# Flipping the first layer's input before its norm: the gain in the copies, the roots behind the projections

## The chip, the cores and the metric

The kernel runs on one core of a Trainium2 chip. A core has TensorE (matrix products into PSUM, weights loaded by LDWEIGHTS), VectorE, ScalarE, GpSimd, and SyncE, which here only issues transfers. The metric is the device time of one execution in microseconds; lower is better.

## What is computed

Two layers of a decoder trunk on 256 tokens of width 1024, in float32. Only the front of layer 0 is touched:

```python
def rms_norm(x, g):
    xf = x.astype(jnp.float32)
    y = xf * lax.rsqrt(jnp.mean(xf * xf, axis=-1, keepdims=True) + EPS)
    return (y * g.astype(jnp.float32)).astype(x.dtype)
...
def hybrid_mixer(h, positions, w_in, ...):
    u = h @ w_in
    ...
    a_out = stick_breaking_attention(sb[:, :, 0], sb[:, :, 1], sb[:, :, 2])
    b_out = conformer_conv(cv[..., :CV_WIDTH], cv[..., CV_WIDTH:], ...)   # val * sigmoid(gate), then a convolution
    q = rope(dl[:, :, 0], positions)
    k = rope(dl[:, :, 1], positions)
    c_out = dilated_mixture(q, k, dl[:, :, 2])
    return jnp.concatenate([a_out, b_out, c_out], axis=-1) @ w_out
...
    for l in range(DEPTH):
        y = hybrid_mixer(rms_norm(h, mix_norm_pre[l]), positions, w_in[l], ...)
        h = h + rms_norm(y, mix_norm_post[l])
        ...  # cross-attention into 256 memory tokens, then a gated ConvFFN
```

The norm's factor splits in two: a root per token and a gain per feature.

## The kernel before

Each engine has its own hand-written program; they meet by semaphores, and each runs its program strictly in the order written. Weights come as 512 KB groups (128 x 1024) through a ring of four: SyncE loads `raw`, ScalarE copies it to `whi` (rounded, L567), VectorE makes `wlo = raw - whi` (L993), and TensorE forms every product in three passes: high by high, high weights by low input, low weights by high input. ScalarE and VectorE run three groups ahead of TensorE, and a group's slot is free again when TensorE has used it.

The start of layer 0, for token tile 0 and then 1 (128 tokens each): ScalarE sums the squares (`squares_x`, L579), VectorE and GpSimd make the root (`st(S_HRS + t)`, one value per partition, since tokens lie on the partitions), TensorE spreads the gain over the partitions by two products (L1626), VectorE multiplies x by root and gain (`first_scale`, L1070), TensorE transposes the result by halves of 512 features (`flip`, L1595) so that features lie on the partitions, ScalarE copies the high part out of PSUM (`first_input_hi`, L589) and VectorE subtracts for the low part (`first_input_lo`, L1075). `idle_products` (L1620) are products of zeros whose result nobody reads. Then come 24 calls of `first_pass` of two products each (L1858), the projection for the dilated q (weight groups 0 to 3).

After it TensorE works through the convolution's value and gate (features on partitions, `transposed_product`, L1665 to L1667; groups 4 to 7), half of the memory's keys (8 to 11), the dilated k and v (`product`, L1648 to L1650; 12 to 19), the stick-breaking q and k (features on partitions, 20 to 23) and v. Between them VectorE prepares the memory, the angles (`angles`), the gated value (L1336, after ScalarE's sigmoid L759), rotates q and k (`rope`, L1218 to L1224), and runs the convolution's 31 taps per half (`conv_taps`, L1273) whenever nothing else is due. The stick-breaking q and k leave PSUM through ScalarE (`transposed_in`, L675) into `sbT`, and `sb_scores` (L1813) uses them next. TensorE's transposes of the convolution (L1968) wait for the last taps.

## Time and profile before

| | us |
|---|---|
| median of three runs | 821.71 |
| lowest, highest | 821.61, 821.96 |
| profiled execution, its span | 820.0 |
| outside its span, by the median | 1.7 |
| TensorE busy | 809.4 |
| VectorE busy | 654.8 |
| ScalarE busy | 528.0 |
| GpSimd busy | 29.2 |

The profile is one execution; the times of its rows count from the start of its span. An engine's busy time is no bound by itself: what counts is which wait ends last in each stretch. A row's duration is that of one instruction or of several merged ones ("x4"); neighbours on an engine overlap by some hundredths of a microsecond. In brackets stands how long the engine was idle before the row, and what released it.

### The profile page before, as it was taken

To read this page: it belongs to the slowest core of one execution; us is meant where nothing else is said; L and a number is where in the kernel's file an instruction comes from. 1 tells how busy PE (TensorE), PEld (TensorE's weight loads), DVE (VectorE), ACT (ScalarE), POOL (GpSimd) and SP (SyncE) were. 2 spreads that over 40 slices of the span, in tenths; PEclk is the share of its full clock that TensorE was granted. 3 is DMA by queue.
4 is the path that set the end of the run, shared out by engine and by line. 5 is a ranking of instruction groups with operands and counts; after the bars stand their busy time and mean duration, and the time that the engine had idled before them with its cause. 6 is when DMAs were issued, how large, how long until landed. Compare 5 with 4: busy or idle time off the path is not lost.

```text
span 820.0 us, 12147 instructions
## 1 busy us (share of the span) xinstructions
PE 809.4 (99%) x4636; PEld 698.3 (85%) x4636; DVE 654.8 (80%) x1149; ACT 528.0 (64%) x823; POOL 29.2 (4%) x54
## 2 busy tenths in 40 slices
PE   8999999999999999999999999999999999999997
PEld 5998888889888888888899889888988888888885
DVE  6899996777776899998387999948788489999753
ACT  5656886567556777765365588756766477776541
POOL 2100000010010000000010000001000000000000
PEclk9999999999999999999999999999999999999999
DMA  8755345473464566556656443456635545555651
GB/s 298 284 178 182 103 129 167 142 259 101 155 233 140 167 206 196 178 191 214 197 201 237 147 154 108 137 168 208 202 121 178 190 129 180 193 176 196 228 184 52
DMA packets 40446, 145.72 MB, mean 178 GB/s; under 512 B 4594, under 2 KB 4738, under 8 KB 40388
## 3 DMA queue, kind: packets, MB, share of 16 engines
q1 hardware_dynamic: 38448, 138.38, 51.4%
q0 software_dynamic: 1936, 6.55, 2.3%
q8 instruction: 37, 0.61, 0.3%
q14 instruction: 21, 0.17, 0.1%
q10 hardware_dynamic: 4, 0.00, 0.0%
HBM read 143.87 MB, written 1.05 MB: 177 GB/s over the span
## 4 chain that ended last, share of the span: by engine, by line
PE 87%; DVE 7%; ACT 3%; issue 1%; DMA 0%; DVEq 0%; POOLq 0%; POOL 0%; ACTq 0%
PE acc L1682 8%; PE psCD L1682 4%; PE acc L1648 4%; PE acc L1649 4%; PE acc L1650 4%; PE acc L1692 4%; PE psAB L1682 4%; PE acc L1745 3%; PE psAB L1648 3%; PE psAB L1650 3%; PE psAB L1649 3%; PE acc L1747 3%; PE acc L1746 3%; PE psCD L1595 3%; PE acc L1665 3%; PE acc L1666 2%
## 5 line engine op out<-in xcount | busy, mean ns | idle before, releaser
L993 DVE TENSOR_TENSOR wlo<-raw,whi 128x1024 fp32r<-128x1024 f32 x240 | 288.1, 1222 | 68.7 <-ACT whi L567 67.1
L567 ACT ACTIVATE whi<-raw 128x1024 fp32r<-128x1024 f32 x240 | 249.4, 1057 | 119.3 <-PE acc L1650 44.1
L1682 PE MATMUL acc<-xT,whi 128*128 128x512 f32 x288 | 89.0, 390 | 0.0
L1682 PEld LDWEIGHTS acc<-xT,whi 128*128 128x128 f32 x288 | 54.1, 188 | 11.8
L1536 DVE SCALAR_TENSOR_TENSOR KT<-V,par,KT 128x255 f32<-128x255 f32 (+1 forms) x144 | 60.0, 480 | 2.1 <-ACT KT L926 1.5
L1692 PE MATMUL acc<-xT,wlo 128*128 128x256 f32 x288 | 58.0, 283 | 0.0
L1273 DVE SCALAR_TENSOR_TENSOR arena<-arena,par 128x256 f32<-128x256 f32 x120 | 50.3, 481 | 0.8 <-ACT arena L767 0.8
L1665 PE MATMUL acc<-xT,whi 128*128 128x256 f32 x176 | 50.9, 289 | 0.0
L1682 PE MATMUL psCD<-xT,whi 128*128 128x512 f32 x160 | 50.0, 393 | 0.0
L1666 PE MATMUL acc<-xT,whi 128*128 128x256 f32 x176 | 49.7, 283 | 0.0
L1667 PE MATMUL acc<-xT,wlo 128*128 128x256 f32 x176 | 49.7, 283 | 0.0
L494 POOL TENSOR_TENSOR stat<-stat 128x1 f32<-128x1 f32 x30 | 18.8, 626 | 775.9 <-DVE stat L1133 401.3
L1692 PEld LDWEIGHTS acc<-xT,wlo 128*128 128x128 f32 x288 | 44.8, 191 | 0.0
L1682 PE MATMUL psAB<-xT,whi 128*128 128x512 f32 x128 | 39.7, 391 | 0.0
L926 ACT ACTIVATE KT<-V,par 128x256 f32<-128x256 f32 x72 | 37.3, 595 | 0.7 <-DVE V L1522 0.7
L1665 PEld LDWEIGHTS acc<-xT,whi 128*128 128x128 f32 x176 | 33.6, 191 | 2.9 <-issue 2.7
L617 ACT ACTIVATE junk<-acc 128x512 bf16<-128x512 f32 x20 | 11.8, 592 | 37.0 <-PE acc L1766 22.6
L1648 PE MATMUL psAB<-whi,gT 128*128 128x512 f32 x88 | 34.2, 389 | 0.0
L1649 PE MATMUL psAB<-wlo,gT 128*128 128x512 f32 x88 | 34.2, 389 | 0.0
L1650 PE MATMUL psAB<-whi,gT 128*128 128x512 f32 x88 | 34.2, 389 | 0.0
L1666 PEld LDWEIGHTS acc<-xT,whi 128*128 128x128 f32 x176 | 33.7, 191 | 0.1
L1667 PEld LDWEIGHTS acc<-xT,wlo 128*128 128x128 f32 x176 | 33.7, 191 | 0.0
(328 smaller groups left out, 2084.8 us busy)
## 6 DMA issues: line engine op xcount, KB each, us to landing
raw<-stream_dram SPq DMA_DIRECT2D x256, 512.0 KB, 4.2
gpost<-gain_dram POOLq DMA_DIRECT2D x6, 512.0 KB, 5.3
gpre<-gain_dram POOLq DMA_DIRECT2D x5, 512.0 KB, 6.2
memn<-mem_dram SPq DMA_DIRECT2D x2, 512.0 KB, 10.3
out_dram<-h SPq DMA_DIRECT2D x4, 256.0 KB, 2.0
cst<-const_dram SPq DMA_DIRECT2D x1, 896.0 KB, 6.1
h<-x_dram SPq DMA_DIRECT2D x2, 256.0 KB, 2.8
h<-x_dram SPq DMA_DIRECT2D x1, 512.0 KB, 8.2
```

Of the source, the lines that this page charges most:

```text
L567: act.activation(home(g)[0], raw[:, s * GW:(s + 1) * GW], ACT.Copy).then_inc(w_hi.sem, 1)
L993: dve.tensor_tensor(lo, raw[:, cols], hi.bitcast(F32), ALU.subtract).then_inc(w_lo.sem, 1)
L1273: e = dve.scalar_tensor_tensor(acc, src, w, acc, ALU.mult, ALU.add)
L1536: e = dve.scalar_tensor_tensor(y[:, c, shift:SEQ], u[:, 0:SEQ - shift], par[:, PC_FW + 3 * fc + 1 - k:PC_FW + 3 * fc + 2 - k], y[:, c, shi ...
L1648: pe.matmul(outs[t], a_hi, whi[:, cols], start=k == 0, stop=False)
L1649: pe.matmul(outs[t], a_hi, wlo[:, cols], start=False, stop=False)
L1650: e = pe.matmul(outs[t], a_lo, whi[:, cols], start=False, stop=k == k_of - 1)
L1665: pe.matmul(dst, whi[:, cols], hi[:, toks], start=k == 0 and c % 2 == 0, stop=False)
L1666: pe.matmul(dst, whi[:, cols], lo[:, toks], start=False, stop=False)
L1667: e = pe.matmul(dst, wlo[:, cols], hi[:, toks], start=False, stop=k == KC - 1 and c % 2 == 1)
L1682: e = pe.matmul(up_halves(j, c), whi[:, cols], both, start=k == 0, stop=k == KC - 1)
L1692: e = pe.matmul(up_halves(j, c)[:, 0:SEQ], wlo[:, cols], hi, start=False, stop=False)
```

## The change

TensorE transposes x itself, neither scaled by the root nor by the gain. The gain comes in as 8 rows of 128, is turned into eight columns by one small product, and each column (one value per feature, so per partition) is the scale of a copy of 128 columns: four scaled copies on ScalarE and four scaled subtractions on VectorE take the place of one each. The roots are put in behind the projections: as a scale per partition where tokens lie on partitions (the dilated v and the stick-breaking v, by ScalarE's copies; the dilated q and k, by angles that VectorE scales beforehand), and as a row spread over all partitions where features do. That row is made by VectorE (`roots_diagonal`), TensorE (`spread_roots`) and VectorE again (`root_row`); VectorE multiplies the gate by it before the sigmoid and the value after, and GpSimd multiplies all of `sbT` by it. The squares of x move behind the first four weight splits. SyncE issues the first weight group second, ScalarE issues the constants' head, and there are seven and five idle products where there were four and two. TensorE's order in the first passes changes too. Layer 1 stays as it was.

```diff
...
+        root_row = gpre[:, 0:SEQ]
+        trig0 = gpre[:, SEQ:SEQ + TOK * 2 * HALF]
+        gain0 = gpre[:, SEQ + TOK * 2 * HALF:SEQ + TOK * 2 * HALF + KC]
+        by_token = lambda n: root_row.unsqueeze(1).to_broadcast([P, n, SEQ])
...
+            def first_rows(n):
                 sp_.dma_start(h[:, n * NT:(n + 1) * NT], x[0:P, n * NT:(n + 1) * NT]).then_inc(x0_in[n].sem, 16)
-            sp_.dma_start(cst[:, 0:CC_TRI], consts[:, 0:CC_TRI]).then_inc(head_in.sem, 16)
+
+            first_rows(0)
             group(0)
+            first_rows(1)
...
-                pool.wait_ge(xn_ready.sem, xn_ready.at(l, 2 * TOK))
+                if l:
+                    pool.wait_ge(xn_ready.sem, xn_ready.at(l, 2 * TOK))
+                else:
+                    pool.wait_ge(root_row_in.sem, 1)
+                    pool.wait_ge(sbT_raw.sem, 2)
+                    pool.tensor_tensor(sbT, sbT, by_token(4), ALU.mult).then_inc(sbT_in.sem, 2)
+                    pool.wait_ge(gpad_in.sem, 1)
+                    pool.wait_ge(k_roped.sem, TOK)
+                    pool.wait_ge(sbT_in.sem, 2)
                 gain(gpre, gpre_in, l, X_PRE)
...
+                act.wait_ge(gain0_cols.sem, 1)
                 act.wait_ge(xt_tr.sem, 2 * t + b + 1)
-                act.activation(x_chunks(0, b, t), blocks(psCD[b]), ACT.Copy).then_inc(xt_hi.sem, 1)
-
-            act.wait_ge(gain0_room.sem, 1)
-            act.dma_start(gain0[0:2, :], gains[0, MIX_PRE, :].rearrange("(n c) -> n c", n=2)).then_inc(gain0_in.sem, 16)
+                for c in range(4):
+                    e = act.activation(x_chunks(0, b, t)[:, c], blocks(psCD[b])[:, c], ACT.Copy,
+                                       scale=gain0[:, 4 * b + c:4 * b + c + 1])
+                e.then_inc(xt_hi.sem, 1)
+
+            act.dma_start(gain_rows, gains[0, MIX_PRE, :].rearrange("(k p) -> k p", p=P)).then_inc(gain0_in.sem, 16)
+            act.dma_start(cst[:, 0:CC_TRI], consts[:, 0:CC_TRI]).then_inc(head_in.sem, 16)
             act.wait_ge(half_set.sem, 1)
             own.link(act.activation(junk[:, 0:1], st(S_POW), ACT.Sin))
-            squares_x(0)
+            first_input_hi(0, 0)
             split_group(0, 0)
+            first_input_hi(0, 1)
+            split_group(0, 1)
             for b in range(2):
-                first_input_hi(0, b)
-            split_group(0, 1)
-            squares_x(1)
+                first_input_hi(1, b)
             split_group(0, 2)
             split_group(0, 3)
-            for b in range(2):
-                first_input_hi(1, b)
+            squares_x(0)
...
-                act.activation(sig, accs[1][1][:, :], ACT.Sigmoid).then_inc(cv_sig.sem, 1)
+                if l:
+                    act.activation(sig, accs[1][1][:, :], ACT.Sigmoid).then_inc(cv_sig.sem, 1)
+                else:
+                    act.wait_ge(gate_scaled.sem, 1)
+                    act.activation(sig, sig, ACT.Sigmoid).then_inc(cv_sig.sem, 1)
...
-                    act.activation(dlv[:, t * NT:(t + 1) * NT], accs[1][t][:, :], ACT.Copy).then_inc(dlv_in.sem, 1)
+                    if not l:
+                        act.wait_ge(h_rs.sem, t + 1)
+                    act.activation(dlv[:, t * NT:(t + 1) * NT], accs[1][t][:, :], ACT.Copy,
+                                   scale=1.0 if l else st(S_HRS + t)).then_inc(dlv_in.sem, 1)
...
-                act.activation(sbv, accs[1][0][:, :], ACT.Copy).then_inc(sbv_in.sem, 1)
+                for t in range(TOK):
+                    rows_t = slice(t * SB_W, (t + 1) * SB_W)
+                    e = act.activation(sbv[:, rows_t], accs[1][0][:, rows_t], ACT.Copy, scale=1.0 if l else st(S_HRS + t))
+                e.then_inc(sbv_in.sem, 1)
...
-            def first_scale(t, n):
-                cols = slice(t * D + n * NT, t * D + (n + 1) * NT)
-                dve.wait_ge(gain0_spread.sem, n + 1)
-                dve.wait_ge(h_rs.sem, t + 1)
-                dve.scalar_tensor_tensor(xn[:, cols], h[:, cols], st(S_HRS + t),
-                                         psAB[n], ALU.mult, ALU.mult).then_inc(xn_ready.sem, 1)
-
             def first_input_lo(t, b):
                 dve.wait_ge(xt_hi.sem, 2 * t + b + 1)
-                dve.tensor_tensor(x_chunks(1, b, t), blocks(psCD[b]), x_chunks(0, b, t).bitcast(F32),
-                                  ALU.subtract).then_inc(xt_lo.sem, 1)
-
-            norm_input(0, 0, 0)
-            for n in range(2):
-                first_scale(0, n)
+                for c in range(4):
+                    e = dve.scalar_tensor_tensor(x_chunks(1, b, t)[:, c], blocks(psCD[b])[:, c],
+                                                 gain0[:, 4 * b + c:4 * b + c + 1],
+                                                 x_chunks(0, b, t)[:, c].bitcast(F32), ALU.mult, ALU.subtract)
+                e.then_inc(xt_lo.sem, 1)
+
+            def roots_diagonal(t):
+                dve.wait_ge(head_in.sem, 16)
+                dve.wait_ge(h_rs.sem, t + 1)
+                dve.tensor_scalar(diag[:, t * P:(t + 1) * P], ident, st(S_HRS + t), None,
+                                  ALU.mult).then_inc(diag_set.sem, 1)
+
+            def first_angles_scaled():
+                dve.wait_ge(trig_ready.sem, 1)
+                for t in range(TOK):
+                    cols = slice(2 * t * HALF, 2 * (t + 1) * HALF)
+                    own.link(dve.tensor_scalar(trig0[:, cols], trig[:, cols], st(S_HRS + t), None, ALU.mult))
+
+            dve.wait_ge(gain0_tr.sem, 1)
+            dve.tensor_copy(gain0, psAB[0][:, 0:KC]).then_inc(gain0_cols.sem, 1)
+            dve.wait_ge(gain0_cols.sem, 1)
+            first_input_lo(0, 0)
             split_group(0, 0)
-            first_input_lo(0, 0)
+            first_input_lo(0, 1)
             split_group(0, 1)
-            norm_input(0, 0, 1)
-            first_input_lo(0, 1)
-            for n in range(2):
-                first_scale(1, n)
+            for b in range(2):
+                first_input_lo(1, b)
             split_group(0, 2)
             split_group(0, 3)
-            for b in range(2):
-                first_input_lo(1, b)
+            for t in range(TOK):
+                norm_input(0, 0, t)
...
+                        roots_diagonal(t)
...
+                    dve.wait_ge(root_spread.sem, 1)
+                    dve.tensor_copy(root_row, psAB[1][:, 0:SEQ]).then_inc(root_row_in.sem, 1)
...
-                dve.wait_ge(cv_sig.sem, cv_sig.at(l, 1))
-                dve.tensor_tensor(gpad[:, :, CV_K - 1:CV_K - 1 + SEQ],
-                                  accs[1][0][:, :].rearrange("p (c n) -> p c n", c=2),
-                                  sig.rearrange("p (c n) -> p c n", c=2), ALU.mult).then_inc(gpad_in.sem, 1)
+                by_half = lambda a: a.rearrange("p (c n) -> p c n", c=2)
+                gated_rows = gpad[:, :, CV_K - 1:CV_K - 1 + SEQ]
+                if l:
+                    dve.wait_ge(cv_sig.sem, cv_sig.at(l, 1))
+                    dve.tensor_tensor(gated_rows, by_half(accs[1][0][:, :]), by_half(sig), ALU.mult).then_inc(gpad_in.sem, 1)
+                else:
+                    dve.wait_ge(root_row_in.sem, 1)
+                    dve.wait_ge(w_used.sem, w_used.at(l, g_cv + PER_TILE))
+                    dve.tensor_tensor(by_half(sig), by_half(accs[1][1][:, :]), by_token(2), ALU.mult).then_inc(gate_scaled.sem, 1)
+                    own.link(dve.tensor_tensor(gated_rows, by_half(accs[1][0][:, :]), by_token(2), ALU.mult))
+                    dve.wait_ge(cv_sig.sem, cv_sig.at(l, 1))
+                    dve.tensor_tensor(gated_rows, gated_rows, by_half(sig), ALU.mult).then_inc(gpad_in.sem, 1)
...
+                    first_angles_scaled()
                     rope(0, qr, g_dlq + PER_TILE, q_roped)
...
-            def first_input(b):
-                pe.wait_ge(xn_ready.sem, b + 1)
-                flip(psCD[b], xn[:, b * NT:(b + 1) * NT]).then_inc(xt_tr.sem, 1)
+            def first_input(t, b):
+
+                pe.wait_ge((x1_in if t else x0_in[b]).sem, 16)
+                if t:
+                    pe.wait_ge(xt_lo.sem, b + 1)
+                flip(psCD[b], h[:, t * D + b * NT:t * D + (b + 1) * NT]).then_inc(xt_tr.sem, 1)
 
             def idle_products(n):
 
                 for i in range(n):
-                    pe.matmul(accs[1][0][:, :], idle[:, 0:P], idle[:, :], start=True, stop=True)
-
-            idle_products(4)
-            pe.wait_ge(spread_set.sem, 1)
+                    pe.matmul(accs[1][0][:, :], idle[:, :], idle[:, :].unsqueeze(1).to_broadcast([P, NT // P, P]),
+                              start=True, stop=True)
+
+            def spread_roots():
+
+                pe.wait_ge(ones_set.sem, 1)
+                for t in range(TOK):
+                    pe.wait_ge(diag_set.sem, t + 1)
+                    e = pe.matmul(psAB[1][:, t * P:(t + 1) * P], ones0, diag[:, t * P:(t + 1) * P], start=True, stop=True)
+                e.then_inc(root_spread.sem, 1)
+
+            idle_products(7)
+            pe.wait_ge(head_in.sem, 16)
             pe.wait_ge(gain0_in.sem, 16)
-            for n in range(2):
-                pe.matmul(psAB[n], pick[:, n * P:(n + 1) * P], gain0, start=True,
-                          stop=True).then_inc(gain0_spread.sem, 1)
-            pe.wait_ge(head_in.sem, 16)
-            first_input(0)
-            idle_products(2)
-            first_input(1)
+            pe.matmul(psAB[0][:, 0:KC], gain_rows, ident[0:KC, 0:KC], start=True, stop=True).then_inc(gain0_tr.sem, 1)
+            first_input(0, 0)
+            idle_products(5)
+            first_input(0, 1)
...
                     first_pass(both_hi, 0, 0)
+                    first_pass(low_x, 0, 0)
                     first_pass(low_w, 0, 0)
-                    first_pass(low_x, 0, 0)
                     first_pass(both_hi, 1, 0)
                     first_pass(low_x, 1, 0)
                     first_pass(low_w, 1, 0)
+                    for b in range(2):
+                        first_input(1, b)
                     first_pass(both_hi, 2, 0)
                     first_pass(low_x, 2, 0)
-                    first_pass(both_hi, 3, 0)
-                    first_pass(low_x, 3, 0)
-                    inputs(0, 1)
                     first_pass(both_hi, 0, 1)
                     first_pass(both_hi, 1, 1)
                     first_pass(low_w, 2, 0)
+                    first_pass(both_hi, 3, 0)
+                    first_pass(low_x, 3, 0)
+                    first_pass(both_hi, 2, 1)
                     first_pass(low_w, 3, 0)
-                    first_pass(both_hi, 2, 1)
                     first_pass(both_hi, 3, 1)
...
+                    spread_roots()
                     transposed_product(g_cv + 2, 2, X, acc[1], k0=4)
+                    pe.wait_ge(root_row_in.sem, 1)
...
```

How the order of instructions moves, at three places (line numbers are those of each version; the names are the code's, `acc0` and `acc1` being the two PSUM sets; what an instruction waits for stands in brackets).

ScalarE, at the start; before:

```order
L579 ACTIVATE junk,stat<-h 128x512 [waits x0_in1]
L567 ACTIVATE whi<-raw 128x1024 [waits w_used,raw_in0]
L589 ACTIVATE xT<-psCD 128x4x128 [waits xt_tr] x2
L567 ACTIVATE whi<-raw 128x1024 [waits w_used,raw_in1]
L579 ACTIVATE junk,stat<-h 128x512 [waits x1_in] x2
L567 ACTIVATE whi<-raw 128x1024 [waits w_used,raw_in2]
L567 ACTIVATE whi<-raw 128x1024 [waits w_used,raw_in3]
L589 ACTIVATE xT<-psCD 128x4x128 [waits xt_tr] x2
```

and after:

```order
L612 ACTIVATE xT<-psCD,gpre 128x128 [waits xt_tr,gain0_cols,act_chain]
L612 ACTIVATE xT<-psCD,gpre 128x128 x3
L588 ACTIVATE whi<-raw 128x1024 [waits w_used,raw_in0]
L612 ACTIVATE xT<-psCD,gpre 128x128 [waits xt_tr,gain0_cols]
L612 ACTIVATE xT<-psCD,gpre 128x128 x3
L588 ACTIVATE whi<-raw 128x1024 [waits w_used,raw_in1]
L612 ACTIVATE xT<-psCD,gpre 128x128 [waits xt_tr,gain0_cols]
L612 ACTIVATE xT<-psCD,gpre 128x128 x3
L612 ACTIVATE xT<-psCD,gpre 128x128 [waits xt_tr,gain0_cols]
L612 ACTIVATE xT<-psCD,gpre 128x128 x3
L588 ACTIVATE whi<-raw 128x1024 [waits w_used,raw_in2]
L588 ACTIVATE whi<-raw 128x1024 [waits w_used,raw_in3]
```

The copies of token tile 1 stood behind the splits of groups 2 and 3 and now stand ahead of them; the squares are gone from this piece. On TensorE, after, the transposes of tile 1 (L1647) that these copies wait for stand behind the products with the low weights of group 1:

```order
L1919 MATMUL acc0<-whi,xT 128x512 [waits xt_hi,w_hi]
L1919 MATMUL acc0<-whi,xT 128x512
L1919 MATMUL acc0<-whi,xT 128x512 [waits xt_lo,w_hi]
L1919 MATMUL acc0<-whi,xT 128x512
L1919 MATMUL acc0<-wlo,xT 128x512 [waits xt_hi,w_lo]
L1919 MATMUL acc0<-wlo,xT 128x512
L1647 MATMUL psCD<-cst,h 128x128 [waits xt_lo,x1_in]
L1647 MATMUL psCD<-cst,h 128x128 x3
L1647 MATMUL psCD<-cst,h 128x128 [waits xt_lo,x1_in]
L1647 MATMUL psCD<-cst,h 128x128 x3
L1919 MATMUL acc0<-whi,xT 128x512 [waits xt_hi,w_hi]
```

Before, they stood behind the products with the high weights of group 3.

VectorE, at the gate of the convolution; before:

```order
L993 TENSOR_TENSOR wlo<-raw,whi 128x1024 [waits w_hi,par_in]
L1336 TENSOR_TENSOR arena<-acc1,arena 128x2x256 [waits cv_sig]
L993 TENSOR_TENSOR wlo<-raw,whi 128x1024 [waits w_hi]
L1218 TENSOR_TENSOR arena<-acc0,trig 128x512 [waits w_used,trig_ready]
L1219 TENSOR_TENSOR arena<-acc0,trig 128x512
```

and after:

```order
L1025 TENSOR_TENSOR wlo<-raw,whi 128x1024 [waits w_hi,par_in]
L1386 TENSOR_TENSOR arena<-acc1,gpre 128x512 [waits w_used,root_row_in]
L1387 TENSOR_TENSOR arena<-acc1,gpre 128x2x256
L1389 TENSOR_TENSOR arena<-arena 128x2x256 [waits cv_sig,dve_chain]
L1025 TENSOR_TENSOR wlo<-raw,whi 128x1024 [waits w_hi]
L1116 TENSOR_SCALAR gpre<-trig,stat 128x64 [waits trig_ready]
L1116 TENSOR_SCALAR gpre<-trig,stat 128x64 [waits dve_chain]
L1257 TENSOR_TENSOR arena<-acc0,gpre 128x512 [waits w_used,trig_ready,dve_chain]
L1258 TENSOR_TENSOR arena<-acc0,gpre 128x512
```

On ScalarE, after, the table load for the sigmoid has a wait for the first of them:

```order
L588 ACTIVATE whi<-raw 128x1024 [waits w_used,raw_in2]
L777 ACTIVATE trig<-trig 128x128 [waits trig_arg]
L788 ACT_TABLE_LOAD [waits gate_scaled]
L788 ACTIVATE arena<-arena 128x512 [waits w_used]
L588 ACTIVATE whi<-raw 128x1024 [waits w_used,raw_in3]
```

One product became three, with ScalarE's sigmoid between the first and the last, and two scalings of angles stand ahead of the rotation (L1257).

GpSimd, ahead of the load of the next gains; before:

```order
L490 DMA par<-param_dram 128x246
L491 DMA pww<-pw_dram 128x512
L487 DMA gpost<-gain_dram 128x1024 [waits mem_gains_tr]
L487 DMA gpre<-gain_dram 128x1024 [waits xn_ready]
L494 TENSOR_TENSOR stat<-stat 128x1 [waits ln_ms] x2
```

and after:

```order
L503 DMA par<-param_dram 128x246
L504 DMA pww<-pw_dram 128x512
L500 DMA gpost<-gain_dram 128x1024 [waits mem_gains_tr]
L544 TENSOR_TENSOR arena<-arena,gpre 128x1024 [waits sbT_raw,root_row_in]
L500 DMA gpre<-gain_dram 128x1024 [waits sbT_in,k_roped,gpad_in]
L507 TENSOR_TENSOR stat<-stat 128x1 [waits ln_ms] x2
```

A product of 128 x 1024 on `sbT` is new, and the load behind it waits for it, for the rotated k and for the gated value, since it overwrites the roots' row and the scaled angles.

## Rows read from the trace of the kernel before

**Rows 1.** The page, busy times: engine, us, share of the span, instructions.
```profile
PE 809.4 (99%) x4636; PEld 698.3 (85%) x4636; DVE 654.8 (80%) x1149; ACT 528.0 (64%) x823; POOL 29.2 (4%) x54
```

**Rows 2.** Stretches: length, busy us (instructions) per engine, granted clock, DMA share, GB/s.
```profile
50.00:100.00 50.00, 50.00 (x332) 42.64 (x331) 48.15 (x149) 35.36 (x67) 0.00 (x0) 1.00 0.48 157
```

**Rows 3.** Timeline, TensorE: start us, us, engine line op out<-in, count [idle before].
```profile
1.94 1.49 PE L1620 MATMUL acc<-idle 128*128 128x512 f32 x3
...
2.37 1.06 PE L1620 MATMUL acc<-idle 128*128 128x512 f32 x2
...
7.73 1.06 PE L1595 MATMUL psCD<-cst,xn 128*128 128x128 f32 x4
...
10.11 0.71 PE L1858 MATMUL acc<-whi,xT 128*128 128x512 f32 x2
...
23.01 0.61 PE L1858 MATMUL acc<-wlo,xT 128*128 128x512 f32 x2
23.46 0.61 PE L1858 MATMUL acc<-whi,xT 128*128 128x512 f32 x2
```

**Rows 4.** The chain that ended last: start us, us, what.
```profile
123.21 0.49 DVE arena L1273
123.74 0.55 PE psCD L1968 x3
```

**Rows 5.** Groups of ScalarE by shape: busy us, mean ns | idle before.
```profile
L669 ACT ACTIVATE xT<-psCD 128x512 fp32r<-128x512 f32 x20 | 10.9, 597 | 19.3 <-PE psCD L1595 19.3
...
L696 ACT ACTIVATE arena<-arena,stat 128x128 f32<-128x128 f32 x8 | 3.2, 402 | 3.1 <-DVE stat L1250 3.1
```

**Rows 6.** SyncE's issues in the timeline; DMA: KB each, median us to landing.
```profile
1.65 0.42 SPq L463 DMA_DIRECT2D cst<-const_dram  x1
...
3.06 0.43 SPq L459 DMA_DIRECT2D h<-x_dram  x1
...
cst<-const_dram SPq DMA_DIRECT2D x1, 80.0 KB, 3.5
...
h<-x_dram SPq DMA_DIRECT2D x1, 512.0 KB, 8.2
```

**Rows 7.** Timeline, ScalarE, the splits of the first groups.
```profile
8.27 1.06 ACT L567 ACTIVATE whi<-raw 128x1024 fp32r<-128x1024 f32 x1 [3.36 <-DMA raw<-stream_dram]
...
13.06 1.99 ACT L567 ACTIVATE whi<-raw 128x1024 fp32r<-128x1024 f32 x2
```

**Rows 8.** Timeline, ScalarE and VectorE, around the gate and the rotation of q.
```profile
39.11 1.28 ACT L759 ACT_TABLE_LOAD   x1
...
36.26 0.42 DVE L1008 TENSOR_SCALAR arena<-cst,arena 128x64 f32<-128x64 f32 x2
...
41.03 0.69 DVE L1336 TENSOR_TENSOR arena<-acc,arena 128x512 f32<-128x512 f32 x1 [0.54 <-ACT arena L759]
...
46.90 0.42 DVE L1224 TENSOR_TENSOR arena<-arena 128x256 f32<-128x256 f32 x1
```

**Rows 9.** Timeline, TensorE's flip of q; VectorE's maxima; the next scores.
```profile
49.15 1.04 PE L1595 MATMUL psCD<-cst,arena 128*128 128x128 f32 x8
...
76.66 0.17 DVE L1237 TENSOR_SCALAR stat<-stat 128x2 f32<-128x2 f32 x1
...
77.09 0.27 PE L1793 MATMUL psAB<-arena 64*128 64x128 f32 x1
```

**Rows 10.** Timeline, ScalarE's copies of q and k, TensorE's first use.
```profile
94.76 1.09 ACT L675 ACTIVATE arena<-acc 128x512 f32<-128x512 f32 x2
...
96.19 0.71 PE L1813 MATMUL psAB<-arena 64*128 64x256 f32 x4
```

**Rows 11.** Groups of GpSimd by shape: busy us, mean ns | idle before.
```profile
L494 POOL TENSOR_TENSOR stat<-stat 128x1 f32<-128x1 f32 x30 | 18.8, 626 | 775.9 <-DVE stat L1133 401.3 <-DVE stat L1415 202.1 <-DVE stat L1169 117.5
...
L497 POOL MEMSET idle<- 128x512 f32 x1 | 0.5, 529 | 0.0
...
L496 POOL MEMSET stat<- 128x1 f32 x1 | 0.1, 98 | 0.3 <-POOLq L2245 0.3
```

38 lines of the change are left out of this document (21 added, 17 removed).

## The prediction

> **What bounds the kernel now.** I read the page's busy times first, then the stretches, then the timelines of the first 50 us by engine, then the chain. TensorE is busy for 99% of the span [rows 1], so a change elsewhere counts only where it moves an instruction for which TensorE waits. VectorE is the other engine to watch: in 50 to 100 us it is busy for 48.15 of 50 us, as TensorE is for all 50 [rows 2]. In the timeline of TensorE the reader is to see that it has slack only at the start. The first pass, 48 products of 512 columns, goes from 10.11 us to 23.9 us, 0.45 behind the start of its last row; at the pace of its last rows (0.45 us for two, 0.227 for one) the 48 need 10.9 us and the eight transposes between them some 1.0 us, so about 2 us of it is waiting or a low clock [rows 3]. From there on TensorE has no idle time that a faster start would not simply shift. The chain shows the second tight place: at 123.7 us TensorE's transposes of the convolution start at the very end of VectorE's last taps [rows 4]. What delays VectorE before that delays the end.
>
> **Part 1, the start.** Removed: the spreading products, the first scaling, and the squares of x from between the weight splits. Added: each copy of a flipped half is four scaled copies of 128 columns. The copy of 512 columns takes 0.60 us; a scaled one of 128 columns takes 0.40 from SBUF [rows 5]. Neighbours overlap by about 0.09, and a source in PSUM saves about 0.03, so four cost 3 x 0.28 + 0.37, and push the next one back by 1.12 us where a plain copy took 0.50.
>
> The constants' head was issued at 1.65 us and took 3.5 us [rows 6]. ScalarE no longer waits for a memset before its issues, so I put this one at about 1.3 and its landing at 4.8 (4.2 at best). Seven idle products, 0.43 apart [rows 3], fill TensorE until about 4.3 from 1.1, the memset before them being shorter. The gain's small product and four transposes at the low clock (four took 1.06 [rows 3], some 0.85 up to the next) give 6.0 for the first flip. Then ScalarE goes: copies until 7.1, split of group 0 (1.06 for one, 0.96 as a step [rows 7]) until 8.1; its weights are issued about 1 us sooner and land about then, where ScalarE had waited 3.36 us for them until 8.27 [rows 7]. The flip of half 1 stands behind five idle products: 6.0 + 2.1 + 0.85 = 8.95 at the low clock, 7.6 at the high one. Copies, then the split of group 1: done at 11.1 (10.3).
>
> Here is the step that decides. ScalarE must now do both copies of token tile 1 before it splits group 2, and TensorE flips that tile only after the low weights of group 1: VectorE's subtraction 1.22, two products 0.45, four transposes 0.45. So ScalarE is idle for about 2.1 us, until 13.2 (12.4), then 2 x 1.12 of copies and 0.96 of split: group 2 at 16.4 (15.6), where it was ready at 14.1 [rows 7]. Behind it stand 36 products in the new order, 36 x 0.227 = 8.2. The first pass ends at 24.6 (23.8) against 23.9: **+0.5 us**. A floor that no shorter step lifts is the landing of x's second tile, issued at 3.06 and landed 8.2 later, at 11.26 [rows 6]; issued 0.5 sooner it gives 10.8 + 0.4 + 2.24 + 1.06 + 8.2 = 22.9, or -1.0. The ceiling is +1.2.
>
> **Part 2, the gate.** Before, the table load and the sigmoid followed the sine, and VectorE's gating product started at 41.03 [rows 8]. Now ScalarE first waits for VectorE's scaled gate, and the table load (1.28) stands behind that wait. VectorE had been idle for 0.54 by then [rows 8], and with the overlap of neighbours could have started at 40.40; now it is 0.35 later, for the copy of the roots' row (256 columns; a row of that size takes 0.42 [rows 8]). So: 40.75 + 0.69 for the scaled gate, 1.28, 0.63 for the sigmoid (512 columns, as a plain copy, and from SBUF), small gaps: gating at 43.44, 2.4 us later than before. The scaled value half hides in that wait. The two scalings of the angles cost 0.42, as two of 64 columns do [rows 8]. VectorE is **2.8 us late** at the end of the rotation of q, whose last row starts at 46.90 and takes 0.42: 47.32 becomes 50.1, while TensorE flips q at 49.15 [rows 8, 9]. Two products that spread the roots are also on TensorE, 0.3 to 0.6 us (its eight transposes take 1.04 [rows 9]); they are covered by this lag. The lag doesn't go away: VectorE has no idle time up to 75 us. It reaches TensorE in steps, at the latest at the score products, where the maxima end at 76.83 and the product that waits for them starts at 77.09 [rows 9]: slack 0.2. Term: **+2.6 us**. If the table load ran ahead of its wait, 1.3 us less: lower bound 1.3, upper 2.8. The roots' diagonals hide in idle time of VectorE before 28 us.
>
> **Part 3, the stick-breaking scores.** GpSimd multiplies the transposed q and k, 128 x 1024, after ScalarE's copies and before TensorE may use them. The copies end at 95.85, TensorE's first use is at 96.19 [rows 10]: slack 0.34. No such operation is in the trace. On GpSimd a 128x1 product takes 0.63 on average, and a memset of 512 columns 0.43 more than one of a single column, so 0.86 per 1024 elements for one stream [rows 11]. One stream would give 1.5, three (two reads, a write) 3.2; I take two reads as the pace: 2.35. Less the slack: **+2.1 us**, bounds 1.1 and 2.9. Behind the wait stand the scores, the value products, a flip and all of the second half of k's memory product; VectorE's mask and ScalarE's softplus wait for the scores, then come the taps whose end TensorE awaits at 123.7 [rows 4]. So it is paid in full.
>
> The Trainium skill (GPSIMD Engine Reference, Performance versus the Vector engine) gives 4497 ns for a two-input product of 2048 columns on GpSimd, by which this one would be an estimated 2.25 us and the sum 0.1 us smaller. The same page (Specifications) says that GpSimd's way to SBUF is contended by VectorE instructions with two SBUF inputs, as the taps are; no row here shows it.
>
> **Part 4.** Scaled copies of v in two pieces, on ScalarE's stretch of the chain: **+0.2 us**. The scaled dilated values cost as much and are covered by VectorE's split. The load of the next gains goes later, to about 100 us, and is wanted at 156.
>
> **Sum.** 0.5 + 2.6 + 2.1 + 0.2 = 5.4 on a span of 820.0. The median of the runs is 821.7, so 1.7 lies around the profiled span. That gives 827.1; I say 827.0.
>
> **Rivals.**
> 1. *The start pays.* If the first copies are fast and the second tile comes early, the split of group 2 follows group 1 directly, ScalarE's order alone gives 13.1 to 13.4 for it, and the pass ends at 21.3 to 21.6, 2.5 us sooner. This rival also needs the later waits hidden, up to the spreading products: 821.7 - 2.5 + 0.45 = 819.7. Against it: the floor of 22.9 above. It wins only if the later waits add less than 0.8 us.
> 2. *One of the two waits is covered.* Either the lag of VectorE or the product on GpSimd is worth little, the start is even or better: 821.7 + 2.1 + 0.2 - 0.5 = 823.5, or within 0.2% with a start of -1.0.
> 3. *TensorE falls to its low clock* while it is idle from 13.7 to 16.4. In the trace a product of 512 columns is 0.43 from the next at the start and 0.227 later [rows 3], the paces of the two levels, 1.2 and 2.4 GHz; the low one lasted to about 10 us, and TensorE is nowhere idle for so long afterwards. Eight to sixteen slow products: 1.6 to 3.2 us more, 829.5. The Trainium skill (TensorE: Matmul & The Clock Gate, What's actually happening) says that the throttled state is the default and activity releases it; by that this idle time could bring it back.
>
> **How the numbers follow.** The forecast holds 0.60, the one-wait-covered case 0.20 (half of it within 0.2%), the start that pays 0.10, low clock 0.07, and 0.03 for no difference by other ways. Faster by over 0.2% is below 820.1, slower is above 823.4; 0.2% is about what a measurement of this kernel can tell from no change. Faster 0.10, same 0.13, slower 0.77. The range: my low bounds give -1.0 + 1.3 + 1.1 + 0.1 = 1.5, or 823.2, and I go on to 822.0 for part of the second case; the high ones 1.2 + 2.8 + 2.9 + 0.3 = 7.2, or 828.9, and with a little of the third 829.3. Below it lies about 0.14, above it 0.05.
>
> **What would show it.** Right: group 2's split on ScalarE starts after 14.5; TensorE's last first-pass product ends at 23.5 to 25; the second table load starts right behind VectorE's scaled gate, at about 41.5; the flip of q waits for VectorE; TensorE waits about 2 us for GpSimd near 100 us; VectorE's last taps end at 127 to 129. Wrong: a first pass that ends before 22.5; a product on GpSimd under 1 us; or idle time of VectorE between 50 and 120 us that swallows the lag.

## The result

The changed kernel takes **830.75 us** (median of 6 runs, 829.70 to 835.64) against 821.66 of the kernel before: a ratio of 1.0122, 95% interval 1.0107 to 1.0136. Four more runs of it, beside other kernels, gave 831.12 to 833.94, ratio 1.0136 (1.0122 to 1.0150). It is slower by 9 us or more, where +5.3 was forecast, and above the range's end of 829.3. The profiled execution took 829.70 us, with a span of 827.7 against 820.0: **+7.7 us**. So there are two things to explain: 7.7 us in a trace where 5.4 were summed, and other runs that are 0.1 to 6 us longer than the one in that trace.

### The profile page after: what moved, and what is told of

Same layout as the page of the kernel before. It is cut to its first block, busy times and chain, and to the rows that moved or that the text cites. A ratio compares the mean times of both kernels' runs of the same rounds, so it can differ in the third digit from the quotient of the medians.

```text
span 827.7 us, 12197 instructions
## 1 busy us (share of the span) xinstructions
PE 810.8 (98%) x4644; PEld 700.9 (85%) x4644; DVE 657.4 (79%) x1161; ACT 531.1 (64%) x837; POOL 31.7 (4%) x55
## 4 chain that ended last, share of the span: by engine, by line
PE 78%; DVE 13%; ACT 5%; issue 2%; DMA 0%; POOL 0%; ACTq 0%; DVEq 0%; POOLq 0%
PE acc L1743 8%; DVE wlo L1025 5%; PE psCD L1743 4%; PE acc L1753 4%; PE psAB L1743 4%; PE acc L1709 4%; PE acc L1710 4%; PE acc L1711 4%; PE acc L1806 3%; PE psAB L1711 3%; PE psAB L1709 3%; PE psAB L1710 3%; PE acc L1808 3%; PE acc L1807 3%; DVE arena L1312 3%; PE psCD L1753 2%
## 5 line engine op out<-in xcount | busy, mean ns | idle before, releaser
L1312 DVE SCALAR_TENSOR_TENSOR arena<-arena,par 128x256 f32<-128x256 f32 x120 | 52.4, 498 | 0.8 <-ACT arena L796 0.8
```

Of the source, the lines that this page charges most:

```text
L1312: e = dve.scalar_tensor_tensor(acc, src, w, acc, ALU.mult, ALU.add)
```

## The profile after

The page's busy times of the changed kernel first (engine, us, share, instructions); [rows 1] answers to it.

```profile
PE 810.8 (98%) x4644; PEld 700.9 (85%) x4644; DVE 657.4 (79%) x1161; ACT 531.1 (64%) x837; POOL 31.7 (4%) x55
```

TensorE has 1.4 us more work than before, so most of the 7.7 us is idle time. Three stretches of the changed kernel show where (length, busy us of TensorE, its weight loads, VectorE, ScalarE and GpSimd, granted clock, DMA share, GB/s); [rows 2] answers to the second.

```profile
0.00:50.00 50.00, 44.37 (x277) 39.31 (x278) 33.37 (x72) 32.23 (x58) 6.51 (x16) 1.00 0.69 247
50.00:100.00 50.00, 49.45 (x316) 41.55 (x314) 48.20 (x145) 33.12 (x62) 0.00 (x0) 1.00 0.49 154
100.00:140.00 40.00, 37.31 (x263) 32.36 (x262) 36.62 (x64) 29.45 (x41) 4.31 (x4) 1.00 0.44 135
```

The same stretches of the kernel before, the first and the third:

```profile
0.00:50.00 50.00, 47.41 (x293) 39.93 (x293) 37.67 (x69) 31.07 (x48) 7.31 (x17) 1.00 0.73 261
...
100.00:140.00 40.00, 39.93 (x256) 34.47 (x255) 33.32 (x56) 31.25 (x40) 1.11 (x2) 1.00 0.49 146
```

TensorE's idle time grew by 3.0 us in the first, 0.55 in the second, 2.6 in the third. The granted clock is 1.00 in all of them. For the opening 10 us that column is to be read with care: in both kernels it gives 1.00, while the products of 512 columns there stand 0.43 us or more apart and later ones 0.227. What level the opening runs at is seen from the pace of its products.

**The start**, in the changed kernel's timeline of TensorE (start us, us, engine line op, tiles, count [idle before]):

```profile
5.82 1.11 PE L1647 MATMUL psCD<-cst,h 128*128 128x128 f32 x4
6.59 2.48 PE L1675 MATMUL acc<-idle 128*128 128x512 f32 x5
8.87 1.05 PE L1647 MATMUL psCD<-cst,h 128*128 128x128 f32 x4
...
14.08 1.04 PE L1647 MATMUL psCD<-cst,h 128*128 128x128 f32 x8
17.95 2.11 PE L1919 MATMUL acc<-whi,xT 128*128 128x512 f32 x8 [2.83 <-ACT whi L588]
```

and of ScalarE and VectorE at the same place:

```profile
11.20 1.13 DVE L1101 SCALAR_TENSOR_TENSOR xT<-psCD,gpre,xT 128x128 fp32r<-128x128 f32 x4 [0.62 <-ACT xT L612]
...
14.77 2.18 ACT L612 ACTIVATE xT<-psCD,gpre 128x128 fp32r<-128x128 f32 x8 [2.66 <-PE psCD L1647]
...
16.79 2.05 ACT L588 ACTIVATE whi<-raw 128x1024 fp32r<-128x1024 f32 x2
```

ScalarE stands idle for 2.66 us until tile 1 is flipped, copies it, and only then splits group 2; TensorE waits 2.83 us for that and goes on at 17.95. The first product behind the first pass, which started at 23.91 before, starts at 26.24: **+2.3 us**.

**The gate**: ScalarE, then VectorE, of the changed kernel; [rows 8] answer to it.

```profile
43.21 1.28 ACT L788 ACT_TABLE_LOAD   x1 [1.67 <-DVE arena L1386]
...
42.45 0.68 DVE L1386 TENSOR_TENSOR arena<-acc,gpre 128x512 f32<-128x512 f32 x1
...
45.24 0.69 DVE L1389 TENSOR_TENSOR arena<-arena 128x512 f32<-128x512 f32 x1 [1.51 <-ACT arena L788]
...
51.62 0.42 DVE L1263 TENSOR_TENSOR arena<-arena 128x256 f32<-128x256 f32 x1
```

The gating product starts 4.2 us later than before (41.03) and the rotation of q ends 4.7 later (46.90 is the row before). Of these, 2.0 were there when VectorE came to the gate: its split ahead of it started at 41.30 against 39.27.

**The stick-breaking scores**: ScalarE's copies, GpSimd, TensorE, VectorE; [rows 10] answer to the first and third.

```profile
99.48 1.09 ACT L700 ACTIVATE arena<-acc 128x512 f32<-128x512 f32 x2
...
100.75 2.62 POOL L544 TENSOR_TENSOR arena<-arena,gpre 128x1024 f32<-128x1024 f32 x1 [70.32 <-ACT arena L700]
...
103.52 0.71 PE L1874 MATMUL psAB<-arena 64*128 64x256 f32 x4 [2.54 <-POOL arena L544]
...
100.71 3.74 DVE L1312 SCALAR_TENSOR_TENSOR arena<-arena,par 128x256 f32<-128x256 f32 x4
```

TensorE is 7.3 us late here (103.52, 96.19 before), and 7.7 at the end. Beside GpSimd's product VectorE's four convolution taps took 3.74 us. The same four in the kernel before:

```profile
95.99 1.66 DVE L1273 SCALAR_TENSOR_TENSOR arena<-arena,par 128x256 f32<-128x256 f32 x4
```

## The experiments

All are compared with runs of the kernel before on the same chip (its medians: 821.46 to 821.59). Diffs are against the changed kernel unless said otherwise, and of the long ones only the lines that matter are shown. A median of four to six runs of a kernel whose own runs lie up to 6 us apart settles little by itself; the traces carry most of what follows.

**1. The changed kernel again**, to see whether the scatter belongs to it.

> The changed kernel once more, unedited, with as many runs as can be had beside those of the cures. Theory (TensorE's clock falls behind its two idle stretches in some runs): granted clocks from 0.999 down to 0.992 to 0.996, times from 829 to over 832 us, lower clocks with longer times, median 830.2 to 831.5. Rival (the scatter belonged to the first chip): all runs within 0.6 us of 829.8.

Measured: 832.87 us, clocks 0.994 to 0.997. The theory's mechanism holds, and the median is worse than it said. The clock alone doesn't order the runs (833.94 us at 0.996, 832.70 at 0.994): the landing of the constants, below, is a second part. Its profiled execution took 833.94 us; two places of it show TensorE's granted clock (stretch, length, busy us, clock, DMA share, GB/s):

```profile
18.00:20.00 2.00, 0.68 (x2) 0.77 0.00 0
20.00:22.00 2.00, 2.00 (x6) 0.50 0.13 29
22.00:24.00 2.00, 2.00 (x9) 0.87 0.92 311
...
106.00:108.00 2.00, 1.64 (x14) 0.96 0.00 0
108.00:113.00 5.00, 5.00 (x32) 0.67 0.61 211
```

0.50 is the lower of the two levels, 1.2 GHz. The missing parts sum to (0.23 + 0.50 + 0.13) x 2 = 1.7 us at the first place and 0.04 x 2 + 0.33 x 5 = 1.7 at the second: each is a stretch of about 3.4 us at half clock. Each follows one of the two idle stretches (2.83 and 2.54 us). In the first trace both were idle just as long and the clock stayed at 1.00.

```profile
6.67 0.59 PE L1689 MATMUL psAB<-cst,arena 8*128 8x8 f32 x2 [2.29 <-DMA cst<-const_dram]
...
19.32 3.57 PE L1919 MATMUL acc<-whi,xT 128*128 128x512 f32 x8 [2.83 <-ACT whi L588]
```

These two rows are of the same execution. Eight products take 3.57 us where they took 2.11. And the first product on the constants stands at 6.67, where it stood at 5.30 in the first trace. So 1.4 (constants) + 1.7 + 1.7 = 4.8 on the span of 827.7 gives 832.5; it was 831.9. Such an execution is explained to 0.6 us.

**2. Group 2 split first.** ScalarE (VectorE likewise):

```
             split_group(0, 1)
+            split_group(0, 2)
             for b in range(2):
                 first_input_hi(1, b)
-            split_group(0, 2)
             split_group(0, 3)
```

> The changed kernel with one order turned: ScalarE and VectorE split weight group 2 ahead of tile 1's transposed copies, not behind them. Theory (the start's loss is the wait of TensorE for group 2 at 17.95, 2.83 us idle, and all of it reaches the end): group 2's high part is done by 13.2, TensorE goes on after its flips at 15.2, then waits up to 1 us for group 3 at about 17.9; the first pass ends 2.0 to 2.3 us sooner (24.0 to 24.3 against 26.25) and the kernel takes 1.8 to 2.5 us less than the changed one, 827.4 to 828.0 in the run that is profiled. Rival (VectorE's own chain ahead of the gate sets what follows, the start's gap is covered by it): first pass sooner, but the gate's scaled half starts still near 42.4 and the time moves under 0.5 us. On the spread of the changed kernel's runs (829.7 to 835.6): if it comes of the 2.83 us gap, it shrinks to under 1 us here; if not, it stays.

Measured: 831.14 us (829.90 to 831.98). In its trace:

```profile
14.95 2.29 PE L1919 MATMUL acc<-whi,xT 128*128 128x512 f32 x8
...
24.91 0.39 PE L1726 MATMUL acc<-xT,whi 128*128 128x256 f32 x1 [0.66 <-DVE wlo L1025]
...
102.26 0.99 PE L1874 MATMUL psAB<-arena 64*128 64x256 f32 x4 [2.54 <-POOL arena L544]
```

and its clock there, by stretches:

```profile
102.00:104.00 2.00, 1.74 (x10) 0.64 0.04 8
104.00:106.00 2.00, 2.00 (x11) 0.51 0.66 242
```

The idle stretch at 15 us is gone. The first pass itself ends some 2.0 us sooner, as expected, but the product behind it then waits 0.66 us for VectorE's split, so that 1.3 us are left (24.91 against 26.24). VectorE's scaled gate starts at 41.21, 1.2 sooner, so the rival is out. At the scores TensorE is still 1.3 us ahead of the first trace (102.26 against 103.52). Then the second idle stretch brings half clock, (0.36 + 0.49) x 2 = 1.7 us, and takes the gain back: span 827.9. The median, 0.4 above the changed kernel's first, would have said that the order is worth nothing. The spread fell to 2.1 us and not under 1, since the second idle stretch is still there.

**3. sbT by VectorE.** ScalarE's copies and GpSimd's product go; VectorE, ahead of its taps:

```
+                    for b in range(2):
+                        dve.tensor_tensor(sbT[:, 2 * b:2 * b + 2, :], by_half(accs[0][b][:, :]), by_token(2),
+                                          ALU.mult).then_inc(sbT_in.sem, 1)
                 conv_taps(17, 19)
```

> The changed kernel with the product of sbT and the root row made by VectorE as it reads PSUM (two of 128x512, about 0.67 us each), in place of ScalarE's two copies and GpSimd's product; nothing else changed. Theory (GpSimd's 2.63 us product stands between the projection and the scores, and it slows VectorE's taps beside it from 1.66 to 3.74 us): TensorE's 2.54 us wait at 103.52 goes, the four taps take 1.66 us again, VectorE pays 1.3 us for the products; stick-breaking scores start at about 101.2 to 101.6 instead of 103.5, and the kernel takes 1.5 to 2.5 us less. Rival (VectorE is the bound here, so that 1.3 us more on it eat the gain): under 1.0 us less, with the mask step starting less than 1 us sooner.

Measured: 829.38 us (828.80 to 830.54), 1.4 us under the changed kernel's first median and 3.5 under its second.

```profile
104.43 0.71 PE L1876 MATMUL psAB<-arena 64*128 64x256 f32 x4 [1.14 <-DVE arena L1437]
...
104.20 1.66 DVE L1309 SCALAR_TENSOR_TENSOR arena<-arena,par 128x256 f32<-128x256 f32 x4
```

The wait falls from 2.54 to 1.14 us and the taps take 1.66 again. The start of this execution is late: the constants (first product at 6.03) cost it 0.7 us and a stretch at half clock behind 18 us another 1.7. 828.4 - 2.4 = 826.0, or 1.7 less than 827.7, inside the expected 1.5 to 2.5.

**4. The Sigmoid table ahead of the wait.** ScalarE:

```
+                    own.link(act.activation(junk[:, 0:1], st(S_POW), ACT.Sigmoid))
                     act.wait_ge(gate_scaled.sem, 1)
```

> The changed kernel with one more ScalarE instruction: a Sigmoid of one column ahead of the wait for the scaled gate, so that its table is loaded before. Theory (the gate costs VectorE 1.51 us of idle, most of it ScalarE's 1.28 us table load behind the wait, and VectorE's lag reaches TensorE): the sigmoid starts at about 43.2 instead of 44.5, VectorE's idle time falls to 0.2 to 0.3, and the kernel takes 1.0 to 1.4 us less. Rival (VectorE's lag is covered by other waits by 80 us): the gate's product 1.2 us sooner, the time within 0.3 us of the changed kernel.

Measured: 830.42 us (829.00 to 832.44). In the trace:

```profile
42.40 1.28 ACT L787 ACT_TABLE_LOAD   x1
...
44.81 0.69 DVE L1390 TENSOR_TENSOR arena<-arena 128x512 f32<-128x512 f32 x1 [0.23 <-ACT arena L789]
```

VectorE's idle time is 0.23 us in place of 1.51, as expected. The median moved by 0.3, as the rival said, but that is within the scatter: this alone decides nothing. The profiled execution had both stretches at half clock, and 828.6 - 2 x 1.7 is 825.2, 2.5 less than 827.7. Of it 0.9 is a start that came earlier in this execution (27.08 - 1.7 = 25.4 for the product behind the first pass, against 26.24), which leaves 1.6 for the table. The earlier start is no effect of the edit; it is seen in the idle products between the first two flips:

```profile
6.62 1.41 PE L1676 MATMUL acc<-idle 128*128 128x512 f32 x5
```

In the first trace the same five took 2.48 us: TensorE was at its lower level there and is at the higher one here, with the clock column at 1.00 in both. Of the traces of kernels with the new start, six show the slow form (runs 1, 2, 3, 6, 9 and the first trace) and seven the quick one up to this place (runs 4, 7, 8, 10, 11 and both of 12). From the first product on the constants to group 2 it took 12.65 us in the first trace and 11.27 here, 1.4 us less; in run 9's trace, of the slow form, 12.34, in run 10's, of the quick one, 11.29. So the form alone moves the start by 1.1 to 1.4 us.

**5. GpSimd beside the taps, in the kernel before.** On GpSimd, for layer 0, with a buffer that is loaded afterwards:

```
+                    pool.wait_ge(sbT_in.sem, 2)
+                    pool.tensor_tensor(gpre[:, :], gpre[:, :], gpre[:, :], ALU.mult).then_inc(spare_set.sem, 1)
```

> The kernel before with one thing added: on GpSimd, when sbT is in SBUF, a product of 128x1024 elements in SBUF (a buffer of ones times itself, in place) for which nobody waits but a load of gains that is needed much later; a memset of that buffer comes at about 20 us. Theory (the two engines share access to SBUF): the four taps beside it take 3.0 to 3.8 us in place of 1.66, and VectorE's mask step starts 1.4 to 2.1 us later; of that 0.3 to 2 us reach the end. Rival (the taps in the changed kernel were slow because of something else there): taps 1.66, time of the kernel before within 0.2 us.

Measured: 823.17 us against 821.48, ratio 1.0025 (1.0016 to 1.0034).

```profile
95.92 3.37 DVE L1280 SCALAR_TENSOR_TENSOR arena<-arena,par 128x256 f32<-128x256 f32 x4
95.93 1.89 POOL L532 TENSOR_TENSOR gpre<-gpre 128x1024 f32<-128x1024 f32 x1 [66.91 <-ACT arena L682]
```

Nobody waits for this product, yet the taps take twice as long (3.37 against 1.66) and the kernel 1.7 us more (1.3 to 2.8 by the interval). It reaches the end where TensorE's transposes of the convolution wait for VectorE's last taps: they start at 124.70, after 0.72 us of idle time, and started at 123.35 before. VectorE loses nearly as much (1.71 us) as GpSimd works (1.89). The Trainium skill (GPSIMD Engine Reference, Specifications) names this contention, of VectorE instructions with two SBUF inputs; by that rule, the trace agrees. How much of the 1.7 us reaches the end in the changed kernel, beside TensorE's wait for the same product, can't be told from this run; the changed kernel's trace loses only 0.4 us in all from the scores to the end.

**6. The idle stretches filled.** TensorE, on banks that are written over afterwards:

```
                     for b in range(2):
                         first_input(1, b)
+                    idle_products(12)
...
+                if not l:
+                    for i in range(11):
+                        pe.matmul(psAB[0], xT[:, 0:P], xT[:, 0:NT], start=True, stop=True)
                 pe.wait_ge(sbT_in.sem, sbT_in.at(l, 2))
                 sb_scores(0)
```

> The changed kernel with products into banks that are written over afterwards put into TensorE's two long waits, and nothing else: 12 of 128x512 (0.227 us each at full clock, 2.7 us) behind the flips of tile 1, and 11 (2.5 us) ahead of the wait for sbT. No wait is shortened. Theory (the changed kernel's runs differ, 829.7 to 835.6, because TensorE's clock falls to half behind these idle stretches in some runs and not in others): all runs at a granted clock of 0.998 or more, median 829.3 to 830.3, spread under 0.8 us. Rival (the clock falls for another reason): the spread stays, clocks down to 0.995, median 830.5 or more.

Measured: 829.47 us (828.43 to 829.75), clocks 0.998 and 0.999 in all four. The first trace's time was 829.70, the median of all ten runs of the changed kernel 832.0 (by ratios to the kernel before, 1.0095 here, 1.0122 and 1.0136 there). More work on TensorE made the kernel some 2.5 us faster than that median, without shortening a wait (the scores start at 103.31). So most of the scatter is the clock behind the two idle stretches. The runs still lie 1.3 us apart, more than the 0.8 expected; the landing of the constants and the pace of the opening are still free to vary.

**7. Three cures together** (2, 3 and 4).

> The changed kernel with three edits together: group 2 split ahead of tile 1's copies, sbT scaled by VectorE out of PSUM, and the Sigmoid table loaded ahead of the wait. In the profiles so far each bought 1.1 to 1.6 us in TensorE's times, but those runs also had one or two stretches of 3.2 us in which TensorE was granted 0.50 of its clock behind a wait of 2.5 to 2.8 us, 1.6 us each. Theory (the three terms add, and with both waits gone no run has such a stretch): 825.2 to 826.5 us, the runs within 1.2 us of each other. Rival (the terms hide each other, or the stretches have another cause): over 827.5 us, with granted clocks of 0.995 to 0.997 in most runs as before.

Measured: 826.42 us (824.73 to 826.46), the median as expected, the runs 1.7 us apart and not 1.2; profiled span 824.3 with no stretch at half clock (one of the other runs has a clock of 0.997). The span is 3.4 us under that of the first trace, of the 4.3 that the cures bought singly (1.3 at the start, 1.7 at the scores, 1.3 of VectorE's idle time at the gate): they add, but for 0.9. It is no clean test of the sum, since this execution had the quick opening, and behind it ScalarE waited 0.93 and 1.70 us for weights that landed late, which it did not in the first trace.

**8. Two edits more**, idle_products(2) for 5, and the angles scaled inside the wait for the sigmoid.

> The kernel with the three cures and two small edits more: 2 idle products in place of 5 between the flips of x's first halves, and the two scalings of the angles (0.54 us) made while VectorE waits for the sigmoid. Theory (both stand on the path): 0.4 to 1.2 us less than the kernel with the three cures, 824.3 to 825.8 us; it doesn't reach the kernel before (821.5), since VectorE still makes 1.3 us of gate products and 1.3 us for sbT and ScalarE's and VectorE's scaled copies stay dearer. Rival (fewer idle products lower TensorE's clock in the first passes): a granted clock under 1 in the first 20 us and a time equal or longer.

Measured: 825.25 us (824.70 to 825.97), as expected. VectorE's rotation of q now ends 1.2 us later than before (last row at 48.13, 46.90 before), TensorE's first dilated scores start 0.25 later, the stick-breaking ones 2.4 later (98.61).

**9. The roots left out** on gate, angles and sbT, so that the kernel no longer computes the layer: layer 0 takes the gate's path of the other layer, `trig` in place of `trig0`, and ScalarE's copies serve sbT_in.

> The changed kernel without the roots of layer 0's norm on the gate, on the angles and on sbT (so q, k, the gate and the stick-breaking scores are computed from x without its root; dlv and sbv keep theirs): the instructions that put them in, and the waits for them, are gone; root row and its copy stay. What is left of the change is its start. Theory (start 2.3 us, gate 2.4, sbT 2.5 add up to the 7.7): 823.9 to 825.2 us, with the first pass ending at 26.2 as in the changed kernel and the gate's product some 2.5 us later than before. Rival (what the start loses is covered by a later wait that the kernel before has too): under 822.7 us.

Measured: 825.64 us (825.00 to 826.04), ratio 1.0050 (1.0038 to 1.0063): what is left of the change costs **4.0 us**, a little over the expected end. That is its start, and with it the making of the roots' row and the scaled copies of v, which this kernel keeps. In its trace:

```profile
35.82 1.06 ACT L584 ACTIVATE whi<-raw 128x1024 fp32r<-128x1024 f32 x1 [1.15 <-DMA raw<-stream_dram]
...
44.22 0.69 DVE L1373 TENSOR_TENSOR arena<-acc,arena 128x512 f32<-128x512 f32 x1 [0.95 <-ACT arena L780]
...
99.36 0.71 PE L1857 MATMUL psAB<-arena 64*128 64x256 f32 x4
```

TensorE's flips of q and k and its first dilated scores are each 2.4 us late (51.54, 68.77 and 75.19 against 49.15, 66.38 and 72.80). VectorE is 3.2 late at the gate, and from 80 us TensorE is too: 99.36 is 3.2 behind 96.19. The span is 3.4 us longer. So a late start reaches the end by way of VectorE, and is larger there than on TensorE. Part of it is not the start's: VectorE's split ahead of the gate starts at 42.05 here, against 41.30 in the changed kernel's first trace, because weights landed late (first row).

**10. The root on sbT left out alone.**

> The changed kernel without the root on sbT alone (the stick-breaking scores are computed from x without its root): ScalarE's copies hand sbT to TensorE as in the kernel before, GpSimd multiplies nothing. Theory (the product costs TensorE its wait of 2.5 us and, in part of the runs, a stretch at half clock behind it): 2.5 to 3.6 us less than the changed kernel, 827.1 to 828.2 us; what then remains to the run with all roots left out (825.6) is the gate's, 1.5 to 2.6 us. Rival (TensorE's wait moves to VectorE's chain beside it, which is 5 us late by then): 829.0 us or more.

Measured: 828.04 us (827.14 to 829.65), as expected; 2.7 under the changed kernel's first median, 4.8 under its second. TensorE's wait at the scores is gone and has not moved to VectorE's chain, as the rival had it:

```profile
101.99 0.71 PE L1871 MATMUL psAB<-arena 64*128 64x256 f32 x4
```

The rest to run 9 is the gate and the angles: 828.04 - 825.64 = **2.4 us**, a difference of two medians whose runs lie 2.5 and 1.0 us apart. The traces give nearly the same: TensorE's first dilated scores start at 76.55 in the changed kernel and at 75.19 in run 9, though VectorE came to its split ahead of the gate 0.75 us sooner in the former: 1.36 + 0.75 = 2.1 us.

**11. The start mended, the roots of run 9 left out.**

> The kernel whose roots are left out on the gate, the angles and sbT (same part of the computation missing as in the run with the roots left out), with its start mended as in the cures: group 2 split ahead of tile 1's copies, 2 idle products in place of 5. It asks what flipping x without its norm can give at best, when the roots cost nothing. In the kernel with the cures the first pass ended at 22.8 us against 23.9 of before, but TensorE's next weights came from VectorE, whose lag was 0.5 to 1.2 us at 77 to 83 us. Theory (VectorE and the landing of the weights set what follows, so an early first pass is worth nothing): 821.3 to 822.8 us, the same as before within 0.2%. Rival (the early start reaches the end): 820.8 or less.

Measured: 824.27 us (823.91 to 826.11): neither. The profiled execution, 826.11 us, was the slowest of six:

```profile
6.70 0.38 PE L1672 MATMUL psAB<-cst,arena 8*128 8x8 f32 x2 [2.40 <-DMA cst<-const_dram]
```

```profile
5.00:10.00 5.00, 2.75 (x13) 0.75 0.97 371
10.00:12.00 2.00, 2.00 (x5) 0.50 1.03 422
12.00:14.00 2.00, 2.00 (x6) 0.50 1.04 393
```

These are the start of its timeline and the stretches behind it. The constants came late, TensorE stood idle for 2.40 us and soon after ran at half clock until past 14 us (0.93 in the next two): (0.25 x 5 + 0.50 x 2 + 0.50 x 2 + 0.07 x 2) = 3.4 us lost. Its first pass ended at 24.8, not 22.8. I had reckoned without both. The other five runs, 823.91 to 825.56, have no profile; why they are 2.4 to 4.0 us above the kernel before stays open. No form of this start that was tried was faster than before.

**12. The constants issued by SyncE**, behind x's first half and ahead of the first weight group, alone and with the five edits.

> The changed kernel with the constants issued by SyncE behind x's first half, ahead of weight group 0, not by ScalarE behind the gain rows; nothing else. On ScalarE's queue their landing took 3.8 to 5.3 us in the profiles of eleven kernels with the new start, so that TensorE's first product stood anywhere from 5.21 to 6.70; on SyncE's queue it took 3.4 and 3.5 us in the two profiles of kernels with the old start. Theory (the landing of the constants is what gates the new start, and its spread is the queue's): 3.3 to 3.8 us to landing, first product at 4.8 to 5.2, median 829.0 to 830.6, while the two idle stretches still scatter the runs. Rival (the landing is late because weights and x share the engines, whichever queue issues): 4.0 us or more, and a median above 831.

> The kernel with all five edits (group 2 first, sbT by VectorE, the table ahead, angles in the wait, 2 idle products) and the constants on SyncE's queue as well. Theory (0.2 to 0.8 us off a kernel that stood at 825.25, whose profiled start was already one of the early ones): 824.3 to 825.1 us, runs within 1 us. It stays above the kernel before: VectorE's extra products are still there. Rival (an earlier start meets weights that land later by the constants' place in the queue): 825.3 us or more.

Measured: 831.56 us (830.07 to 832.63) and 825.05 (823.79 to 825.42). The constants' issue landed after 2.6 us in both, and TensorE waits at the next place, the second half of x. In the first of the two:

```profile
4.25 0.38 PE L1689 MATMUL psAB<-cst,arena 8*128 8x8 f32 x2
...
7.79 0.66 PE L1647 MATMUL psCD<-cst,h 128*128 128x128 f32 x4 [1.41 <-DMA h<-x_dram]
...
16.45 2.69 PE L1919 MATMUL acc<-whi,xT 128*128 128x512 f32 x8 [2.83 <-ACT whi L589]
```

```profile
102.00:104.00 2.00, 0.35 (x2) 0.78 0.00 0
104.00:106.00 2.00, 2.00 (x11) 0.50 0.34 96
106.00:108.00 2.00, 2.00 (x12) 0.50 0.47 164
108.00:113.00 5.00, 5.00 (x37) 0.81 0.41 109
```

The landing is shorter than on ScalarE's queue (2.6 against 3.8 to 5.3 us), and shorter than the 3.3 us expected. Whether that is the queue isn't shown: the issue also moved ahead of the first weight group, and in the kernel before, on SyncE's queue behind both halves of x, the same transfer took 3.5. Group 2 starts 1.5 us sooner, with the quick opening in this execution. The time did not follow, and its median is on the rival's side of 831: this execution lost 1.7 us at 18 us and (0.22 + 0.50 + 0.50) x 2 + 0.19 x 5 = 3.4 behind the scores, 5.1 in all. What the earlier constants are worth without that isn't shown.

In the second, the wait for x's second half is long enough to be a third idle stretch:

```profile
8.06 1.11 PE L1650 MATMUL psCD<-cst,h 128*128 128x128 f32 x4 [2.23 <-DMA h<-x_dram]
```

Behind it the clock is 0.79 from 5 to 10 us and 0.67 from 10 to 12, once more 1.7 us. 825.05 is in the expected range, within the scatter of run 8's 825.25, and the lowest median of a kernel that computes all of the layer: 3.6 us behind the kernel before.

## Why the prediction was wrong

**Right:** the direction, the three places, and the mechanism at each. ScalarE idles until tile 1 is flipped and splits group 2 after 14.5 (16.79); the table load follows VectorE's scaled gate (at 43.21, not 41.5); TensorE waits for GpSimd near 100 us. No rival with a gain showed. Three signs missed: the first pass ends at 26.2, not by 25; VectorE's last taps end at 131.3, not by 129; and the flip of q, 2.8 us late at 51.92, has no idle time of TensorE before it: TensorE came there that late by itself, and VectorE's lag met it further on.

**Part 1, the start: the step that failed.** +0.5 was forecast with a ceiling of +1.2; TensorE lost 2.3 in the first trace, and the kernel up to 4.0 (run 9). The idle time of ScalarE in front of tile 1's copies was the right mechanism (2.66 us, 2.1 forecast); the times that lead up to it, and what carries the delay on, were not. Five things in it:
- The flips ended later. The first copies began at 7.06, not 6.0 (the constants 0.5 later, then four transposes of 1.11 from 5.82, and a hop), and the chain group 0, flip, copies, group 1 carried that on.
- VectorE's four low copies step by 1.04 us like ScalarE's. I had charged ScalarE for the split into four, and on VectorE's side counted only the split of the weights, so the low weights of group 1, and with them the flips of tile 1, came about half a microsecond later still. Group 2 was ready to use at 17.95, where 16.4 was the forecast for the end of its split.
- I gave only TensorE's lag as the start's cost. VectorE came 2.0 us late to its split ahead of the gate (2.8 in run 9), and the prediction started it at +0.35.
- The landing of the constants was taken as one number, 4.8. It is a range: TensorE's first product stood at 5.21 to 6.70 in the traces with the constants on ScalarE's queue. That is 1.5 us on the first thing that the new start waits for. TensorE's opening products in the kernel before waited for the gain's load instead (0.76 us at 4.18).
- The level of the opening was given two values, 16.4 for group 2 at the low one and 15.6 at the high one. The traces show both forms, 1.1 to 1.4 us apart (run 4), and the first trace had the slow one. So a part of its 2.3 us is chance: run 4's edit touches nothing before 40 us, and its opening was the quick one.

**Part 2, the gate.** The delay from the split ahead of the gate to the gating product grew by 4.2 - 2.0 = 2.2 us, where 2.4 were summed, and the angles' scalings took 0.54, not 0.42. VectorE's total of 4.7 is this plus the start's 2.0. The term of 2.6 agrees with runs 9 and 10: 2.4 by the medians, 2.1 by the traces. What was wrong is that start and gate were not chained on VectorE: 0.5 + 2.6 = 3.1 on TensorE where 4.7 came out (the first value products start at 90.10 against 85.38).

**Part 3, sbT.** 2.62 us for the product against 2.35, in the bounds; TensorE's wait 2.54. The term of 2.1 measured 2.5 to 2.7 (and 2.35 less the slack of 0.34 is 2.0). The Trainium skill (GPSIMD Engine Reference, Performance versus the Vector engine) has its figure for an addition of 2048 columns, and the estimate from it was 2.25. That lies between this product's 2.62 and the 1.89 of the one in place in run 5, both of them beside VectorE's taps. The contention, which I cited and left out of the sum, is real: it doubles VectorE's taps. But it cost little beyond TensorE's wait: from the scores to the end only 0.4 us were added.

**Part 4** was about right: from the scores (+7.3) to the span (+7.7) 0.4 is left, for 0.2 forecast.

So the trace's 7.7 is 2.3 + 2.4 + 2.6 + 0.4, and the sum was short by the start's 1.8 and the 0.5 of sbT. The working had two slips of its own that decide nothing: the floor of the start adds up to 22.7, not 22.9, and the middle of 24.6 and 23.8 is 0.3 past 23.9, not 0.5. Four scaled copies took 1.14 us where 1.21 was reckoned. The profiled time alone, 829.70, is already past the range's end.

**Rival 3, the low clock, was given 0.07 and is in most runs.** Seven of the ten runs of the changed kernel have a granted clock of 0.997 or less, the other three 0.998 or more and times of 829.7 to 830.2 us. The mechanism was as described and cost 1.7 us each time, as its lower figure of 1.6 said; run 6 is the test of it. It was wrong to make it a rival of the forecast: it comes on top of it. And it has two places, since the wait for GpSimd, 2.5 us long, is a second idle stretch, which I had priced at its length alone. The Trainium skill (TensorE: Matmul & The Clock Gate, What's actually happening) takes the throttled state for the default that activity must release; by that rule, the traces agree. With the low clock added at both places the upper bound would have been 821.7 + 7.2 + 2 x 1.7, or 832.3, which holds the median; five of the ten runs lie above even that, since the start's own ceiling was too low.

The longest run, 835.64, has a clock of 0.992 and no profile. Two stretches and late constants give 834.5 (829.7 + 4.8); a stretch twice as long, as in run 12, would do for the rest, but that execution left no trace to show it.

## What to carry to other kernels

A new wait on TensorE of the length of those here (2.2 to 2.8 us) costs its length and, in a part of the runs, a stretch at half clock behind it: add it to the high end for each wait, and look at the granted clock in short windows, and at the pace of the products in the opening, before reading a small edit's time. Removing a norm from the start bought nothing here, where the constants, the second half of x or the weights landed just behind it, and its factors came back as VectorE work on the engine that was next in line. Carry a delay forward on each engine separately, then take the later one at each meeting point.

## What was not expected of the hardware

- Idle stretches of 2.2 to 2.8 us on TensorE were followed by 0.50 of the clock in some executions and not in others of the same kernel: that of 2.83 us in five of seven traces, that of 2.54 in four of five. Each time cost 1.7 us, and 3.4 in two traces (runs 11 and 12). Filled with products, four of four runs kept 0.998 or more. None of the shorter waits, up to 1.7 us, was followed by it in any trace.
- The opening products ran at the pace of the lower or of the higher level from one execution to the next, 2.48 or 1.41 us for the same five, and the clock column doesn't tell the two apart.
- A two-input product of GpSimd in SBUF (1.89 us in place on 1024 columns, 2.62 with a row repeated) stretched four taps of VectorE beside it from 1.66 to 3.37 and 3.74 us.
- The same 80 KB landed 2.6 us after its issue on SyncE's queue, behind one transfer and ahead of the first weights, and 3.8 to 5.3 us after it on ScalarE's, in the same opening microseconds.
